# Multiplying output-projection slots in two 64-row halves of the array

## The chip, the cores and the metric

The kernel runs on one core of a Trainium2 chip. The metric is device time in microseconds (us) for one execution, the median of several runs.

## What is computed

A decoder trunk of four layers over 256 tokens of width 1024. Each layer has a token mixer (layers 0 and 3 a short gated convolution, layer 1 retention, layer 2 a chunked spatial gating), then a mixture of 16 experts of which each token uses two, then a gated embedding. All three mixers end in an output projection, a matrix product whose result is added to the layer's input:

```python
# layer 1, retention: VDIM = 2048 rows of w_out
o = o.reshape(bsz, seq, RET_VDIM).astype(x.dtype)
return (jax.nn.silu(g) * o) @ w_out
...
# layer 2, spatial gating: 3072 rows of w_out
vs = jnp.einsum("gts,bnsgd->bntgd", ws, v) + b_s.T[None, None, :, :, None]
return (u * vs.reshape(bsz, seq, SGU_HALF)) @ w_out
...
x = _layer_norm(ALPHA * x + mix, ln_g[i, 0], ln_b[i, 0])
ffn = _moe(x, router_w, router_b, moe_w_gate[i], moe_w_up[i], moe_w_down[i])
```

## The kernel before

**Tiling.** Tokens stand in two tiles of 128 (`T` = 2). Dense weights come in slots of 1 MB: 128 partitions by four quarters of 512 columns. A slot of an output projection holds 256 rows of `w_out`, as two chunks `j` of 128 rows, by 1024 columns, as two halves `c` of 512; quarter `2*j + c` is chunk `j`, half `c`. The retention layer's projection has 8 slots, the gating layer's 12, a convolution layer's 4.

**Precision by two parts.** Activations and weights are split into a high and a low part of type fp32r (`w_hi`, `w_lo`; for activations the pairs of views `oT`, `uvT`, `gT` in the buffer that the profile calls `work_r`). `product` (lines 635 to 639) makes one product from three matmuls: high by high (L637), high activation by low weight (L638), low activation by high weight (L639). The stationary operand is a 128x128 block of the activations, the moving one a quarter of the slot. The profile shows their types as f32.

**Sums.** The projection has four sums that run over all slots: PSUM bank `2*t + c` for token tile `t` and column half `c`. `rows_slot` works through one slot for one tile: 4 quarters x 3 matmuls. It starts the sums in slot 0 and ends them in the last slot, where it raises `half_done` and `mix_done`; for the second tile it raises `weights_used` with its last matmul, which frees the slot for the loads, casts and residues of later slots (SP, ScalarE L1248, VectorE L1556).

**Order.** The order on TensorE is written out by hand. In the retention layer (`retention_mixer`): slot 0 for both tiles, `rows_both` for slots 1 and 2, slot 3 for tile 0, transposes of later heads, slot 3 for tile 1, `rows_both` for slot 4, then `last_rows` for slots 5 to 7, tile by tile. In the gating layer (`sgu_mixer`), for q = 0 and 1: slot 4q for both tiles, `rows_both` for slot 4q+1, four spatial products (L927), `rows_both` for slot 4q+2, slot 4q+3 for tile 0, transposes, slot 4q+3 for tile 1; then `rows_both` for slot 8 and `last_rows`. `rows_both` is thus called for eight slots. It runs `rows_slot` for tile 0 and then for tile 1. `slot` (line 630) waits until the slot's low part is there.

**Other matmuls.** The expert products (`pair_product`, L1033) put two experts side by side on two column halves of the array: 64 columns of operand each, results on 64 PSUM partitions each, in plain f32. The gathers (L1025) are full-array matmuls of type fp32r with 256 moving columns. The scatter products (L1043, `put_back`) are full-array fp32r matmuls with 512 columns. L872 is retention's inner product, full-array f32. L648 is the transposes.

Of the kernel before, what the change touches and what calls it, by code (L numbers as in the profile page):

```python
# [5 lines left out]
P = 128  # L6
D = 1024
SEQ = 256
T = SEQ // P
# [16 lines left out]
HALF = 64  # L26
# [159 lines left out]
def build(nc, A, out):  # L186
# [9 lines left out]
    with ctx:  # L196
# [3 lines left out]
        def sem(name):  # L200
            return ctx.enter_context(nc.semaphore(name))
# [64 lines left out]
        psum = ctx.enter_context(nc.psum_tensor("psum", [P, 8, NB], F))  # L266
# [77 lines left out]
        weights_used = sem("weights_used")  # L344
# [2 lines left out]
        xt_in_psum, xt_ready = sem("xt_in_psum"), sem("xt_ready")  # L347
        x_half_ready, x_tile_ready, half_done = sem("x_half_ready"), sem("x_tile_ready"), sem("half_done")
        whole_used = sem("whole_slots_used")
        put_half, general_done = sem("put_half"), sem("general_path_done")  # L350
        norm_row, gate_norm_row, bias_row = sem("norm_row"), sem("gate_norm_row"), sem("bias_row")
        mix_done, mix_read = sem("mix_done"), sem("mix_read")
# [39 lines left out]
        def wait_over(eng, L, engine, step, r, p):  # L392
# [3 lines left out]
            eng.wait_ge(over[L][engine], n * PAIRS * r + n * p + OVER[engine].index(step) + 1)  # L396

        whole_slots = [proj for _, proj, _ in starts]
        places, load_order = zip(*expert_places())
        def expert_slot(L, k):  # L400
# [17 lines left out]
        def split_count(n):  # L418

            return n + 1 - QUICK - sum(proj < n for _, proj, _ in starts)  # L420
# [200 lines left out]
        @block.tensor  # L621
        def _(pe):
            mm = nc.tensor.matmul

            def quarters(n):

                return (w_hi[:, HIGH_OF[n], :].rearrange("p (j n) -> p j n", j=4),
                        w_lo[:, RAW_OF[n], :].rearrange("p (j n) -> p j n", j=4))

            def slot(n):  # L630

                pe.wait_ge(lo_ready, split_count(n))
                return quarters(n)

            def product(out, lhs, rhs, start, stop):

                mm(out, lhs[0], rhs[0], start=start, stop=False)  # L637
                mm(out, lhs[0], rhs[1], start=False, stop=False)  # L638
                return mm(out, lhs[1], rhs[0], start=False, stop=stop)  # L639

            def part(v, *at):
                return [a[at] for a in v]
# [93 lines left out]
            def rows_slot(n, count, lhs, q, t, i, done):  # L736


                s = 4 * q + i
                w = slot(n + s)  # L740
                order = [(j, c) for j in range(2) for c in range(2)]
                if s == count - 1:
                    order = [(j, c) for c in range(2) for j in range(2)]
                for j, c in order:
                    last = product(psum[:, 2 * t + c, :], part(lhs, ALL, 2 * s + j, t),
                                   part(w, ALL, 2 * j + c), s == 0 and j == 0, s == count - 1 and j == 1)
                    if s == count - 1 and (j, c) == (1, 0) and done is not emb_in_psum:
                        last.then_inc(half_done, 1)
                if t == 1:
                    last.then_inc(weights_used, 1)  # L750
                elif s == count - 1:
                    last.then_inc(done, 1)
# [4 lines left out]
                return [a.rearrange("p j (t n) -> p j t n", t=T) for a in v]  # L757

            def rows_both(n, count, lhs, s):
                for t in range(T):  # L760
                    rows_slot(n, count, lhs, s // 4, t, s % 4, mix_done)

            def last_rows(L, n, count, lhs):

# [74 lines left out]
            def retention_mixer(L):  # L839
# [63 lines left out]
                for i in range(1, 3):  # L903
                    rows_both(n, 8, tiled(oT), i)
# [3 lines left out]
                rows_slot(n, 8, tiled(oT), 0, 1, 3, mix_done)  # L908
                pe.wait_ge(oT_ready, 8)
                rows_both(n, 8, tiled(oT), 4)  # L910
                last_rows(L, n, 8, tiled(oT))

            def sgu_mixer(L):
# [35 lines left out]
                for q in range(2):  # L949
                    pe.wait_ge(mt_ready[L], 4 * (q + 1))  # L950
                    for t in range(T):
                        if q == 0:
                            pe.wait_ge(proj_ready[L], block_ready(5, t, 1))
                        rows_slot(n, 12, uvT, q, t, 0, mix_done)
                    rows_both(n, 12, uvT, 4 * q + 1)
                    spatial(q + 2)
                    rows_both(n, 12, uvT, 4 * q + 2)
                    rows_slot(n, 12, uvT, q, 0, 3, mix_done)
                    turn(q + 1)
                    rows_slot(n, 12, uvT, q, 1, 3, mix_done)  # L960
# [574 lines left out]
        def _(dve):  # L1535
# [99 lines left out]
            def layer_norm(t, k, banks_read=None):  # L1635

                rows_at, eps = (lambda c: psum[:, 2 * t + c, :], LN_EPS / ALPHA ** 2) if k % 2 else (
                    lambda c: x[:, t, c * NB:(c + 1) * NB], LN_EPS)

                dve.wait_ge(dve_step, steps[0])  # L1640
                if banks_read is not None:
                    dve.sem_inc(banks_read, 1)
                dve.wait_ge(lnp_loaded, 32 * (k + 1))

                def subtract_mean(i):
                    cols = slice(i * NB, (i + 1) * NB)
                    step(stt(x[:, t, cols], rows_at(i), nmv[:, 0, 0:1], ln_par[:, 0, cols],  # L1647
                             ALU.subtract, ALU.mult))

                [(_, rstd)] = moments([stats[:, t, 0:2, :]], subtract_mean, eps)  # L1650
                dve.wait_ge(dve_step, steps[0])
                for c, ready in enumerate((x_half_ready, x_tile_ready)):
                    cols = slice(c * NB, (c + 1) * NB)
                    stt(x[:, t, cols], x[:, t, cols], rstd, ln_par[:, 1, cols], ALU.mult, ALU.add).then_inc(ready, 1)
# [448 lines left out]
```

## Time and profile before

| | us |
|---|---|
| median of the timed runs | 1615.64 |
| lowest and highest of three | 1615.56, 1615.71 |
| span of the profiled execution, first to last instruction | 1613.2 |
| difference of the median and the span (launch and end) | 2.4 |
| TensorE busy in the span | 1600.2 |
| VectorE busy | 689.4 |
| ScalarE busy | 460.4 |

The profiled execution's own time is not listed beyond its span. A busy time of TensorE counts a matmul from its start to the end of its drain, and the next one starts before that end. The distance of starts tells what one costs. Weight loads have an engine row of their own, PEld.

### The profile page before, as it was taken

What the parts mean: (1) busy time and instruction counts of PE and PEld (TensorE: products, weight loads), DVE (VectorE), ACT (ScalarE), POOL (GpSimd) and SP (SyncE); (2) the same over time, 40 slices, a digit from 0 to 9 for tenths busy, and PEclk for the clock granted to TensorE, in tenths of its full rate; (3) what the DMA queues carried; (4) which work ended last, traced back from release to release, by engine and by line L of the source; (5) the groups of instructions that cost most, each with busy time, mean ns of one, the idle gap of its engine ahead of it and who ended that gap; (6) DMA issues with size and microseconds to landing.
All of it is one profiled execution on the core that took longest, in us unless ns stands there. A gap on an engine that the chain in (4) does not pass through costs nothing.

```text
span 1613.2 us, 17962 instructions
## 1 busy us (share of the span) xinstructions
PE 1600.2 (99%) x7576; PEld 961.3 (60%) x7584; DVE 689.4 (43%) x1023; ACT 460.4 (29%) x557; POOL 46.5 (3%) x47
## 2 busy tenths in 40 slices
PE   9999999999999999999999999999999999999998
PEld 7874433478877744433788888643434887444335
DVE  5671111294757711111956755511115767211117
ACT  5522111154433221111544433211102452211113
POOL 1000000010000000000110000000010000000000
PEclk9999999999999999999999999999999999999999
DMA  6989999946636799999557556999997388999992
GB/s 262 371 368 401 423 420 421 421 176 266 243 132 243 281 414 423 421 421 421 222 200 280 182 205 235 389 397 421 421 420 324 141 343 375 385 422 421 421 421 102
DMA packets 75146, 534.43 MB, mean 331 GB/s; under 512 B 8976, under 2 KB 9136, under 8 KB 10544
## 3 DMA queue, kind: packets, MB, share of 16 engines
q1 hardware_dynamic: 73728, 530.95, 81.2%
q0 software_dynamic: 1328, 2.21, 0.4%
q8 instruction: 65, 1.06, 0.3%
q14 instruction: 25, 0.20, 0.0%
HBM read 532.07 MB, written 1.05 MB: 330 GB/s over the span
## 4 chain that ended last, share of the span: by engine, by line
PE 90%; DVE 6%; DMA 3%; ACT 1%; issue 1%; SPq 0%; DVEq 0%; ACTq 0%
PE psum L1033 39%; PE psum L637 12%; PE psum L639 12%; PE psum L638 12%; PE psum L1025 4%; PE psum L648 3%; PE psum L1043 3%; DVE w_lo L1556 2%; PE psum L982 2%; DMA x<-in_experts 1%; DMA raw<-in_experts 1%; PE psum L975 1%; PE psum L927 1%; PE psum L872 1%; DVE x L1647 0%
## 5 line engine op out<-in xcount | busy, mean ns | idle before, releaser
L1556 DVE TENSOR_TENSOR w_lo<-raw,w_hi 128x2048 fp32r<-128x2048 f32 (+1 forms) x128 | 272.5, 2145 | 187.2 <-ACT w_hi L1248 186.7
L637 PE MATMUL psum<-w_hi,xT_hi 128*128 128x512 f32 x672 | 265.3, 395 | 3.0 <-DVE w_lo L1556 3.0
L1248 ACT ACTIVATE w_hi<-raw 128x2048 fp32r<-128x2048 f32 (+1 forms) x128 | 221.4, 1751 | 155.7 <-PE psum L639 113.1
L639 PE MATMUL psum<-w_hi,xT_lo 128*128 128x512 f32 x672 | 261.8, 390 | 0.0
L638 PE MATMUL psum<-w_lo,xT_hi 128*128 128x512 f32 x672 | 261.6, 389 | 0.0
L1248 ACT ACTIVATE work<-psum 128x512 f32<-128x512 f32 x152 | 85.8, 597 | 349.0 <-PE psum L648 247.3
L637 PEld LDWEIGHTS psum<-w_hi,xT_hi 128*128 128x128 f32 x672 | 126.2, 188 | 30.6 <-DVE w_lo L1556 4.5
L1033 PE MATMUL psum<-raw,xg 128*64 128x512 f32 x624 | 143.8, 594 | 0.0
L639 PEld LDWEIGHTS psum<-w_hi,xT_lo 128*128 128x128 f32 x672 | 126.1, 188 | 26.7
L638 PEld LDWEIGHTS psum<-w_lo,xT_hi 128*128 128x128 f32 x672 | 126.3, 188 | 25.8 <-issue 0.2
L1952 DVE TENSOR_REDUCE cg<-psum 128x1 f32<-128x256 f32 x32 | 13.6, 425 | 233.9 <-PE psum L1103 233.9
L1556 DVE TENSOR_TENSOR work_r<-psum,work_r 128x512 fp32r<-128x512 f32 x52 | 34.5, 688 | 183.7 <-ACT work_r L1248 183.7
L1248 ACT ACTIVATE xg<-psum 128x512 f32<-128x512 f32 x84 | 49.8, 597 | 203.3 <-PE psum L1025 102.1
L1033 PE MATMUL psum<-expert_work,xg 128*64 128x512 f32 x448 | 103.5, 594 | 0.0
L1033 PEld LDWEIGHTS psum<-raw,xg 128*64 128x64 f32 x624 | 43.9, 137 | 84.5 <-issue 83.9
L1033 PE MATMUL psum<-raw,work 128*64 128x512 f32 x400 | 92.9, 593 | 0.5 <-DMA raw<-in_experts 0.3
L637 PE MATMUL psum<-w_hi,work_r 128*128 128x512 f32 x224 | 89.2, 398 | 0.8 <-ACT work L1248 0.8
L639 PE MATMUL psum<-w_hi,work_r 128*128 128x512 f32 x224 | 87.6, 391 | 0.0
L638 PE MATMUL psum<-w_lo,work_r 128*128 128x512 f32 x224 | 87.5, 391 | 0.0
L1033 PE MATMUL psum<-expert_high,xg 128*64 128x512 f32 x336 | 79.5, 594 | 0.0
L1556 DVE TENSOR_TENSOR w_hi<-psum,w_hi 128x512 fp32r<-128x512 f32 x24 | 16.6, 692 | 141.7 <-ACT w_hi L1248 141.7
L1248 ACT ACTIVATE work_r<-psum 128x512 fp32r<-128x512 f32 x52 | 29.4, 600 | 159.7 <-PE psum L1033 156.2
(172 smaller groups left out, 1712.8 us busy)
## 6 DMA issues: line engine op xcount, KB each, us to landing
raw<-in_experts SPq DMA_DIRECT2D x128, 1024.0 KB, 15.9
raw<-in_slots SPq DMA_DIRECT2D x120, 1024.0 KB, 4.9
expert_work<-in_experts SPq DMA_DIRECT2D x88, 1024.0 KB, 15.4
expert_high<-in_experts SPq DMA_DIRECT2D x60, 1024.0 KB, 12.2
expert_spare<-in_experts SPq DMA_DIRECT2D x40, 1024.0 KB, 13.2
expert_bias<-in_experts SPq DMA_DIRECT2D x20, 1024.0 KB, 13.9
x<-in_experts SPq DMA_DIRECT2D x20, 1024.0 KB, 15.6
expert_norm<-in_experts SPq DMA_DIRECT2D x16, 1024.0 KB, 13.7
```

Source lines behind the costliest of these rows:

```text
L637: mm(out, lhs[0], rhs[0], start=start, stop=False)
L638: mm(out, lhs[0], rhs[1], start=False, stop=False)
L639: return mm(out, lhs[1], rhs[0], start=False, stop=stop)
L648: last = nc.tensor.transpose(psum[:, bank, i * P:(i + 1) * P], c, ident[:, :])
L872: last = mm(psum[:, 4 + k % 4, :], sT[:, h, (c + s) * P:(c + s + 1) * P], rv[:, s, h * DV:(h + 1) * DV], start=s == 0, stop=s == c)
L927: mm(tiles(psum[:, 4 + k % 4, 0:SVB]), sgu_wT[:, b // 2, :], sv[:, c, 3 * b:3 * b + 3, :], start=True, stop=True).then_inc(vs_in_psum, 1)
L982: last = mm(psum[:, 2 * t + c, :], pT[:, j, t * P:(t + 1) * P], whole[:, 2 * j + c, :], start=j == 0, stop=j == 1)
L1025: last = mm(psum[:, bank, j * SEQ:(j + 1) * SEQ], x_split[a][:, t, chunk], pick[:, t, Q * SEQ:(Q + 1) * SEQ], start=t + a == 0, stop=t + a ...
L1033: last = mm(psum[columns(e), bank, :], lhs(j, e), w[:, 2 * j + e, :], start=start and j == 0, stop=stop and j == 1)
L1043: last = mm(psum[:, bank0 + 2 * t + c, :], where[:, t * P:(t + 1) * P], what[i][:, c * NB:(c + 1) * NB], start=start and i == 0, stop=stop ...
L1248: return nc.scalar.activation(dst, src, func)
L1556: return tt(lo, whole, hi.bitcast(F), ALU.subtract)
```

## The change

`rows_both` no longer calls `rows_slot`. It splits each product by depth: the upper 64 partitions (rows of the array) and the under 64 are two matmuls with 128 output columns and 512 moving columns each. They are issued in turn, upper, under, upper, under, and at any time the two halves add to different sums (PSUM banks). A slot runs in four groups `k`. In group `k` the upper half adds to sum `k` of the list (c, t) = (0,0), (0,1), (1,0), (1,1), and the under half to sum `(k + 2) % 4`; after four groups every sum has had both halves. New waits keep the two halves from one sum: groups 0, 2 and 3 wait on the new semaphore `halves_done`, which TensorE itself raises at the end of groups 0 to 2, and group 1 waits on `weights_used` of the slot before, which group 3 (or a tile-1 `rows_slot`) raises.

```diff
         whole_used = sem("whole_slots_used")
+        halves_done = sem("row_halves_done")
...
             mm = nc.tensor.matmul
+            halves = [0]
...
             def rows_both(n, count, lhs, s):
-                for t in range(T):
-                    rows_slot(n, count, lhs, s // 4, t, s % 4, mix_done)
+
+                w = slot(n + s)
+                upper, under = slice(0, HALF), slice(HALF, P)
+                sums_of = [(c, t) for c in range(2) for t in range(T)]
+                for k in range(4):
+                    if k == 1:
+                        pe.wait_ge(weights_used, n + s)
+                    elif halves[0]:
+                        pe.wait_ge(halves_done, halves[0] - k // 2)
+                    for j in range(2):
+                        for x_part, w_part in ((0, 0), (0, 1), (1, 0)):
+                            for rows, (c, t) in ((upper, sums_of[k]), (under, sums_of[(k + 2) % 4])):
+                                last = mm(psum[:, 2 * t + c, :], lhs[x_part][rows, 2 * s + j, t],
+                                          w[w_part][rows, 2 * j + c], start=False, stop=False)
+                    if k < 3:
+                        last.then_inc(halves_done, 1)
+                        halves[0] += 1
+                    else:
+                        last.then_inc(weights_used, 1)
```

## Rows read from the trace of the kernel before

**Rows 1.** The page: span, TensorE's busy time, granted clock by slice, the chain's shares.
```profile
span 1613.2 us, 17962 instructions
...
PE 1600.2 (99%) x7576; PEld 961.3 (60%) x7584; DVE 689.4 (43%) x1023; ACT 460.4 (29%) x557; POOL 46.5 (3%) x47
...
PEclk9999999999999999999999999999999999999999
...
PE 90%; DVE 6%; DMA 3%; ACT 1%; issue 1%; SPq 0%; DVEq 0%; ACTq 0%
```

**Rows 2.** Chain that ended last, 500 to 552 us, retention's projection: start, us, what.
```profile
by line: PE psum L639 28.4%; PE psum L637 28.0%; PE psum L638 28.0%; PE psum L872 9.9%; PE psum L648 5.0%; PE psum L982 1.7%
...
500.05 5.15 PE psum L872 x12
...
524.30 1.75 PE psum L648 x16
```

**Rows 3.** Waits of TensorE in the whole run: us in total, times, longest.
```profile
PE psum L637 <- DVE w_lo L1556: 3.0, 6, 0.8
PE psum L669 <- POOL ones L577: 1.0, 1, 1.0
```

**Rows 4.** Groups by line and form: busy us, mean ns of one, idle before.
```profile
L1033 PE MATMUL psum<-raw,xg 128*64 128x512 f32 x624 | 143.8, 594 | 0.0
...
L637 PE MATMUL psum<-w_hi,work_r 128*128 128x512 f32 x224 | 89.2, 398 | 0.8 <-ACT work L1248 0.8
L639 PE MATMUL psum<-w_hi,work_r 128*128 128x512 f32 x224 | 87.6, 391 | 0.0
L638 PE MATMUL psum<-w_lo,work_r 128*128 128x512 f32 x224 | 87.5, 391 | 0.0
```

**Rows 5.** Timeline, TensorE, retention's projection (start, length): first and last of 64.
```profile
509.62 0.39 PE L639 MATMUL psum<-w_hi,work_r 128*128 128x512 f32 x1
...
523.90 0.40 PE L639 MATMUL psum<-w_hi,work_r 128*128 128x512 f32 x1
```

**Rows 6.** Timeline, TensorE, at 644.75 us: two gather matmuls, joint record.
```profile
644.58 0.40 PE L1025 MATMUL psum<-work_r 128*128 128x256 f32 x2
```

**Rows 7.** All gather matmuls: ns of one, least, median and most.
```profile
L1025 PE MATMUL psum<-work_r x512: 277/283/657, 116.0 to 1504.4; 128*128 128x256 f32 x171
```

**Rows 8.** Timeline around 513 us: product matmuls and their weight loads.
```profile
513.02 0.39 PE L639 MATMUL psum<-w_hi,work_r 128*128 128x512 f32 x1
513.03 0.19 PEld L637 LDWEIGHTS psum<-w_hi,work_r 128*128 128x128 f32 x1
513.25 0.39 PE L637 MATMUL psum<-w_hi,work_r 128*128 128x512 f32 x1
```

**Rows 9.** Timeline around 647 us: weight loads of the column halves.
```profile
646.98 0.14 PEld L1033 LDWEIGHTS psum<-expert_high,xg 128*64 128x64 f32 x2 [0.29 <-issue]
647.41 0.14 PEld L1033 LDWEIGHTS psum<-expert_high,xg 128*64 128x64 f32 x2 [0.28 <-issue]
```

**Rows 10.** Timeline, TensorE, 309.3 to 310.2 us: full array, then column halves.
```profile
309.12 0.63 PE L1043 MATMUL psum<-xT_hi,work_r 128*128 128x512 f32 x2
309.68 1.08 PE L1033 MATMUL psum<-expert_high,work 128*64 128x512 f32 x4
```

**Rows 11.** Timeline, 316.2 to 317.4 us: column halves, then full array.
```profile
315.74 1.03 PE L1033 MATMUL psum<-x,work 128*64 128x512 f32 x4
316.69 0.30 PEld L1043 LDWEIGHTS psum<-work_r 128*128 128x128 f32 x2 [0.81 <-issue]
316.70 0.74 PE L1043 MATMUL psum<-work_r 128*128 128x512 f32 x2
...
317.28 0.40 PE L1043 MATMUL psum<-w_hi,work_r 128*128 128x512 f32 x1
```

## The prediction

> **What bounds the kernel now.** I read the page first: TensorE is busy for 99% of the span, the chain that ended last runs on TensorE for 90% of it, and no slice of the span shows less than full granted clock (2.4 GHz) [rows 1]. The time is therefore a sum of TensorE instructions, and a change in a matmul stage is worth what it does to the start-to-start distance of matmuls there. Then I read the chain inside the retention layer's output projection: every piece of it is TensorE [rows 2], and of the few waits that TensorE has in the whole run, the largest total is 3.0 us, 0.8 us at a time [rows 3]. No transfer, cast or copy stands before this stage that could end up setting its length, so a shorter or longer matmul stage is passed on to the end in full.
>
> The busy column is of no use here. One product matmul has a record of 0.39 us [rows 4], but the next one starts after less than that, since matmuls are pipelined. What counts is the distance of starts: 64 product matmuls start between 509.62 and 523.90, so one costs (523.90 - 509.62) / 63 = 0.2267 us [rows 5]. All product matmuls of the output projections, three times 224, have this shape [rows 4].
>
> What is in the 0.2267 us? A gather matmul has the same data type and half the columns (256): two of them have a joint record of 0.40 us [rows 6] and one alone, at the median, of 0.283 [rows 7], so their starts are 0.12 us apart. Twice the columns cost 0.107 us more; 512 columns then take 0.213 us and 0.013 us are left that do not depend on the width. That remainder, a gap at each change of stationary operand, is all that a rearrangement of the same multiplications can win. The weight load itself is hidden already: the load for the next matmul starts at 513.03, with the matmul that began at 513.02, and ends (0.19 us) before the next matmul at 513.25 [rows 8].
>
> **The change, part by part.** It touches only slots that go through rows_both: s = 1, 2, 4 of the retention layer and s = 1, 2, 5, 6, 8 of the gating layer, 8 slots in all. Each has 2 tiles x 4 quarters x 3 products = 24 matmuls now: 24 x 0.2267 = 5.44 us, and 8 slots 43.5 us, 2.7% of the span.
>
> *The matmuls.* Each becomes two of half the depth (64 of 128 partitions), with all 128 output columns and all 512 moving columns: 48 matmuls and 48 loads for a slot, in 24 pairs. A matmul's length is its moving columns, so halving the depth saves nothing by itself; the change lives on both halves of a pair running at once. The trace of before has no 64-row matmul. The nearest rows are the expert products, which split the array by columns (128*64): their loads come in twos at 646.98 and 647.41, so a pair takes 0.43 us [rows 9], and a full-array matmul of the same type takes 5.15 / 12 = 0.43 us too [rows 2]. Two column halves thus run wholly side by side. I take it that row halves do so too. Then a pair has 0.213 us of streaming, plus whatever gap each half has at its own change of operand. Each half still reads one operand and then 512 columns, as the whole array does now, so I keep the gap: 0.2267 us for a pair, 24 pairs a slot, change 0. The bounds: if the gap vanishes, as it seems to have in the column pairs (0.43 us, twice 0.213 for a type that streams at half the rate), 192 pairs x -0.0133 = -2.6 us. If nothing overlaps, 192 x +0.2267 = +43.5 us.
>
> *Going into and out of halves.* The column halves show what it costs to turn the array over. In: a matmul pair of line 1043 begins at 309.12, its second member at 309.12 + 0.63 - 0.40 = 309.35, so the next was due at 309.58; the first column pair comes at 309.68, and the second follows after 1.08 - 0.59 = 0.49 us instead of 0.43 (0.59 is the record of one such matmul [rows 4]). Together 0.10 + 0.06 = 0.16 us [rows 10]. Out: two pairs from 315.74 are through at 316.60, the next full matmul starts at 316.70, and two of them take 317.28 - 316.70 = 0.58 us where 0.46 is usual: 0.10 + 0.12 = 0.22 us, since the next operand can be loaded only after the change [rows 11]. One visit costs 0.38 us. The visits: retention slots 1 and 2 together, slot 4 alone; in the gating layer the spatial products stand between slots 1 and 2 and between 5 and 6, and slot 8 is alone. That is 2 + 5 = 7 visits, 7 x 0.38 = 2.6 us. The lower bound is 0 (row halves might not need the turnover), the upper one is about 0.5 us a visit, 3.5 us, as a 128-column load (0.19 us) must be awaited [rows 8] where the column half awaits a 64-column load (0.14 us) [rows 9].
>
> Here a page bears on it. The Trainium skill ("TensorEngine Tiling (Array Packing)", Key Properties) says that a change of the tiling mode, not of the tile, drains the engine. The column rows agree; no row shows a row split, and by the rule row halves pay as well, whereas without it this term is 0 and the time stays at 1615.6 us.
>
> *The waits.* A slot gets four: on halves_done before groups 0, 2 and 3, on weights_used before group 1. Behind them on TensorE stand only the slot's own matmuls, and behind those the release of the slot. Each asks for the end of the group before the last, and 12 matmuls (6 pairs, 1.36 us) issued in between cover it, against 0.39 us from the start to the end of a group's last matmul [rows 4]. I cost them at nothing. Without that cover one wait would be like a turnover outward, 0.22 us, and the 31 of them (the very first group has none) some 7 us.
>
> *Instruction rate.* A pair needs two loads and two matmuls in 0.2267 us, 0.057 us each. The densest rows are transposes, a load and a matmul in 1.75 / 16 = 0.109 us, 0.055 each [rows 2]; gathers, of the type that matters, need 0.12 us, 0.06 each [rows 6, 7]; two loads started back to back stand 0.30 - 0.19 = 0.11 us apart [rows 11]. This is the tight place, and a rival below.
>
> *What doesn't move.* weights_used still rises once at the slot's end, so raw loads, casts and residues start as now; mix_done and half_done come from slots not touched.
>
> Sum: 0 + 2.6 + 0 = +2.6 us. The profiled execution's span is 1613.2 us, 2.4 us under the median of the timed runs, 1615.64; the stage is added to both alike. **Forecast 1618.2 us**, +0.16%, which is within the 0.2% that a measurement of this kernel can tell from no change.
>
> **The rivals.**
>
> *A. The gap is hidden.* While one half changes its operand the other streams, and a pair takes 0.215 us, half of the 0.43 of a column pair [rows 9]. 192 x -0.0117 = -2.2 us; with the 2.6 us of turnovers 1616.0 us, without them 1613.4. For it: the column pairs show no gap. Against it: the two halves never wait for each other, so a gap in each half lengthens the pair; for that I put A below the forecast. The Trainium skill ("TensorE: Matmul & The Clock Gate", Part 3) has loads overlap with running matmuls only where their row groups differ, which speaks for A as the change alternates row groups. The trace differs from that rule: loads of the same rows overlap now [rows 8].
>
> *B. Loads and matmuls of the two halves queue on one path (slower).* If 0.12 us is not the gather's streaming plus gap but the least distance at which this data type can be loaded and started [rows 6, 7], a pair takes 0.24 us. Against it stand the transposes, whose rate would give 0.219 us for two [rows 2]. It decides as soon as two loads and two starts need more than 0.2267 us. 192 x 0.0133 = +2.6 us on top of the turnovers: 1620.8 us.
>
> *C. The halves don't run at once: the change doesn't do what it says.* The two halves of a pair write two different sums over all 128 partitions at the same time, which the column halves (64 partitions each) never do. If the engine takes them one after the other, 48 matmuls a slot at 0.2267 us add 43.5 us: 1661.7 us.
>
> **How the numbers follow.** Forecast 0.44, A 0.24, B 0.14, C 0.16; 0.02 for something not thought of. Below 1612.4 us would be faster by over 0.2%: even a vanished gap without turnovers (1613.1) does not reach it, so 0.02. Above 1618.9 is slower: B, C and a tenth of the forecast's chance (a turnover of 0.5 us): 0.34. The rest is 0.64. The range takes in A without turnovers and B with slightly dearer ones, 1613.4 to 1621.2, and leaves out C.
>
> **What would show it.** In the timeline of the changed kernel, matmuls of 64*128 in the retention projection: starts in twos with 0.2267 us between twos bear out the forecast, 0.215 A, 0.24 B, and single starts 0.2267 us apart C. The turnover shows where halves meet full matmuls: 0.1 us extra before the first and a first distance lengthened by 0.05 to 0.12. A stretch without a matmul inside a slot would show that a wait lacks its cover. I am wrong if halves do not overlap, or if the turnover of row halves is free.

## The result and the profile after

The changed kernel takes 1620.25 us (median of 16 runs) beside 1615.65 us for the kernel before, and the ratio of the runs on record is 1.0026, 95% interval 1.0018 to 1.0033, that is +4.2 us (2.9 to 5.3; the two medians differ by 4.6). In a second set it took 1619.89 beside 1617.09 us, ratio 1.0022 (1.0011 to 1.0033). It is a little slower, by about 0.2%, and the forecast was 1618.2 us.

The page after: TensorE is still busy for 99% of the span. In the chain VectorE's share has fallen and that of DMA has grown; most of DMA's are expert loads, and one piece of 6.9 us is the slot load that e6 and e7 below are about.

```profile
span 1616.7 us, 18351 instructions
...
PE 1601.8 (99%) x7768; PEld 959.5 (59%) x7776; DVE 686.2 (42%) x1023; ACT 460.5 (28%) x557; POOL 53.2 (3%) x47
...
PE 91%; DMA 5%; DVE 3%; ACT 1%; issue 1%; SPq 0%; ACTq 0%
```

The half matmuls by form (busy us, mean ns of one). 256 + 128 of 64 rows stand in place of 192 of 128 rows; one of them has a record as long as a full one of rows 4, 0.39 us:

```profile
L774 PE MATMUL psum<-w_hi,work_r 64*128 64x512 f32 x256 | 41.5, 393 | 0.7 <-DVE work_r L1575 0.7
...
L774 PE MATMUL psum<-w_lo,work_r 64*128 64x512 f32 x128 | 25.0, 387 | 0.0
```

The timeline of TensorE as the retention projection goes into halves (start, length, count). Compare rows 5 and 10:

```profile
510.03 0.39 PE L640 MATMUL psum<-w_lo,work_r 128*128 128x512 f32 x1
510.26 0.39 PE L641 MATMUL psum<-w_hi,work_r 128*128 128x512 f32 x1
510.58 0.50 PE L774 MATMUL psum<-w_hi,work_r 64*128 64x512 f32 x2
510.91 0.40 PE L774 MATMUL psum<-w_lo,work_r 64*128 64x512 f32 x2
...
513.23 0.62 PE L774 MATMUL psum<-w_hi,work_r 64*128 64x512 f32 x4
513.68 0.39 PE L774 MATMUL psum<-w_lo,work_r 64*128 64x512 f32 x2
513.91 0.62 PE L774 MATMUL psum<-w_hi,work_r 64*128 64x512 f32 x4
514.36 0.39 PE L774 MATMUL psum<-w_lo,work_r 64*128 64x512 f32 x2
514.59 0.62 PE L774 MATMUL psum<-w_hi,work_r 64*128 64x512 f32 x4
```

Each "x2" with a record as long as one matmul's (0.39 us) is a pair: both halves start together. From 513.23 to 514.59 six pairs start, (514.59 - 513.23) / 6 = 0.227 us a pair, what a full matmul took in rows 5. So the pair costs exactly what the whole did; nothing was won and nothing lost there.

And out of halves again, to be read beside rows 11:

```profile
521.16 0.39 PE L774 MATMUL psum<-w_lo,work_r 64*128 64x512 f32 x2
521.39 0.39 PE L774 MATMUL psum<-w_hi,work_r 64*128 64x512 f32 x2
521.70 0.50 PE L639 MATMUL psum<-w_hi,work_r 128*128 128x512 f32 x1
522.04 0.40 PE L640 MATMUL psum<-w_lo,work_r 128*128 128x512 f32 x1
...
524.35 0.40 PE L641 MATMUL psum<-w_hi,work_r 128*128 128x512 f32 x1
```

In: the first pair was due at 510.26 + 0.23 = 510.49 and came at 510.58 (+0.09); the second followed after 0.33 instead of 0.23 (+0.10). Out: due 521.61, came 521.70 (+0.09); the second after 0.34 (+0.11). Then both ways the distance is a little long for a while: the ten starts from 510.91 to 513.23 take 2.32 us and those from 522.04 to 524.35 take 2.31, where 2.27 is usual. This drift is no mark of the split. The kernel before has it behind 16 transposes, where the array stays whole: ten starts in 2.30 us.

```profile
526.12 0.39 PE L638 MATMUL psum<-w_lo,work_r 128*128 128x512 f32 x1
...
528.42 0.39 PE L639 MATMUL psum<-w_hi,work_r 128*128 128x512 f32 x1
```

**Where the time lies.** Both touched stages run from the first product of slot 0 to the first embedding matmul. Those two starts are the rows of the timeline from which every length below is taken. For the kernel before:

```profile
504.64 0.79 PE L637 MATMUL psum<-w_hi,work_r 128*128 128x512 f32 x1
...
551.29 0.59 PE L982 MATMUL psum<-raw,emb 128*128 128x512 f32 x1
...
941.00 0.39 PE L637 MATMUL psum<-w_hi,work_r 128*128 128x512 f32 x1
...
1015.91 0.59 PE L982 MATMUL psum<-raw,emb 128*128 128x512 f32 x1
```

For the changed kernel:

```profile
504.59 0.79 PE L639 MATMUL psum<-w_hi,work_r 128*128 128x512 f32 x1
...
552.96 0.59 PE L1001 MATMUL psum<-raw,emb 128*128 128x512 f32 x1
...
941.86 0.39 PE L639 MATMUL psum<-w_hi,work_r 128*128 128x512 f32 x1
...
1019.06 0.59 PE L1001 MATMUL psum<-raw,emb 128*128 128x512 f32 x1
```

Retention: 46.65 us before, 48.37 after. Gating: 74.91 before, 77.20 after. Together +4.0 us; the rest of the two spans differs by 0.5 us the other way. The same two lengths of every kernel that ran, each from its one profiled execution, beside the median time (us):

| kernel | retention | gating | time | ratio to before, interval |
|---|---|---|---|---|
| before | 46.65 | 74.91 | 1615.65 | |
| changed, first profile | 48.37 | 77.20 | 1620.25 | 1.0026 (1.0018 to 1.0033) |
| changed, second (e0) | 47.63 | 77.21 | 1619.89 | 1.0022 (1.0011 to 1.0033) |
| changed, third (e7) | 48.30 | 77.21 | 1625.95 | one run |
| whole depth (e1) | 46.65 | 74.91 | 1615.85 | 0.9996 (0.9985 to 1.0007) |
| upper halves only (e2) | 47.55 | 77.20 | 1617.73 | one run |
| more visits (e3) | 49.74 | 79.56 | 1624.59 | 1.0044 (1.0028 to 1.0061) |
| halves in blocks (e4) | 48.93 | 80.42 | 1625.64 | one run |
| quarters (e5) | 51.91 | 83.45 | 1635.68 | one run |
| residues first (e6) | 47.61 | 77.21 | 1620.46 | 1.0017 (1.0007 to 1.0027) |

e0, e1, e3 and e6 ran beside 1617.09 us for the kernel before, the single runs beside 1615.16. The total time also carries waits in other stages, which come and go from profile to profile; in e7 and e5 one of 2.6 us, 0.4 us in the others, fell into the last layer. The stage lengths carry one such wait alone (0.7 us in the retention stage, see e6 and e7), so the argument on the split goes by them.

One more stretch differs. Near the end of the last layer, between the last scatter matmul (ended at 1582.59) and the next matmul, TensorE stands idle in the changed kernel:

```profile
1584.28 0.59 PE L656 MATMUL psum<-const 128*128 128x512 bf16 x2 [1.69 <-issue]
```

From the end of that scatter matmul to the end of the span it is 32.43 us in before, e1 and e2, which have as many matmuls as before, and longer in all seven profiles of kernels that have more: 33.2 us in e0, 34.1 in the first profile and 34.4 in e7, all three of the changed kernel, at most 34.5 (e5). So the change seems to cost another 0.8 to 2.0 us there, outside of the stages that it touches. e2 has the split and its turnovers too, so the number of instructions is the likelier cause; but the profile doesn't show what TensorE waited for ("issue"), and no run was made for this question. In the first profile the two stages (+4.0 us) and this stretch (+1.6) come to 5.6 us, and the span grew by 3.5: the rest of it was 2.1 us shorter.

### The profile page after: what moved, and what is told of

It is laid out like the page before. It is cut to its first block, busy times and chain, and to the rows that moved or that the text cites. A ratio compares the mean times of both kernels' runs of the same rounds, so it can differ in the third digit from the quotient of the medians.

```text
span 1616.7 us, 18351 instructions
## 1 busy us (share of the span) xinstructions
PE 1601.8 (99%) x7768; PEld 959.5 (59%) x7776; DVE 686.2 (42%) x1023; ACT 460.5 (28%) x557; POOL 53.2 (3%) x47
## 4 chain that ended last, share of the span: by engine, by line
PE 91%; DMA 5%; DVE 3%; ACT 1%; issue 1%; SPq 0%; ACTq 0%
PE psum L1052 38%; PE psum L639 11%; PE psum L641 11%; PE psum L640 11%; PE psum L1044 4%; PE psum L1062 4%; PE psum L650 3%; PE psum L774 2%; DMA raw<-in_experts 2%; PE psum L1001 2%; PE psum L807 2%; DMA x<-in_experts 1%; DVE w_lo L1575 1%; PE psum L994 1%; DMA raw<-in_slots 1%; PE psum L946 1%
## 5 line engine op out<-in xcount | busy, mean ns | idle before, releaser
L1575 DVE TENSOR_TENSOR w_lo<-raw,w_hi 128x2048 fp32r<-128x2048 f32 (+1 forms) x128 | 269.1, 2119 | 191.1 <-ACT w_hi L1267 190.7
L1575 DVE TENSOR_TENSOR work_r<-psum,work_r 128x512 fp32r<-128x512 f32 x52 | 34.5, 688 | 184.4 <-ACT work_r L1267 184.4
L1044 PE MATMUL psum<-work_r 128*128 128x256 f32 x512 | 74.9, 295 | 0.0
L1044 PEld LDWEIGHTS psum<-work_r 128*128 128x128 f32 x512 | 64.9, 190 | 10.8 <-issue 7.3
L1052 PEld LDWEIGHTS psum<-expert_work,xg 128*64 128x64 f32 x448 | 31.5, 137 | 60.5 <-issue 59.6
```

The lines of the kernel that those rows point to most:

```text
L1044: last = mm(psum[:, bank, j * SEQ:(j + 1) * SEQ], x_split[a][:, t, chunk], pick[:, t, Q * SEQ:(Q + 1) * SEQ], start=t + a == 0, stop=t + a ...
L1052: last = mm(psum[columns(e), bank, :], lhs(j, e), w[:, 2 * j + e, :], start=start and j == 0, stop=stop and j == 1)
L1575: return tt(lo, whole, hi.bitcast(F), ALU.subtract)
```

## The experiments

**e0: the changed kernel once more.**

> The changed kernel once more, for a second profile beside the others of this set. Theory: in the retention layer's projection and in the gating layer's, the stretch from the first product of slot 0 to the embedding matmuls (before: 46.6 us and 62.9 us from the first product of the first slot) is longer than before by 1.0 us (2 visits) and 2.3 us (5 visits), 0.47 us for each visit to row halves. In the first profile the retention stage had grown by 1.7 us, as TensorE also waited 0.7 us there for residues on VectorE, behind a slot load that took 6.9 us. If that wait is chance, it is missing here and the total is 1619.2 us; if it belongs to the change, it is here again and the total is 1620 us.

(The 62.9 us for the gating stage in this text is a slip; by the rows above it is 74.9.) Measured: retention +0.98, gating +2.30 us, no wait before slot 4, 1.0022 in the ratio. So the seven visits (each one into the halves and out again) cost 3.28 us, 0.47 each, and the 0.7 us of the first profile are not always there.

**e1: full depth in the new order.**

```diff
-                            for rows, (c, t) in ((upper, sums_of[k]), (under, sums_of[(k + 2) % 4])):
-                                last = mm(psum[:, 2 * t + c, :], lhs[x_part][rows, 2 * s + j, t],
-                                          w[w_part][rows, 2 * j + c], start=False, stop=False)
+                            c, t = sums_of[k]
+                            last = mm(psum[:, 2 * t + c, :], lhs[x_part][:, 2 * s + j, t],
+                                      w[w_part][:, 2 * j + c], start=False, stop=False)
```

> Full-depth products in the changed kernel's order of sums, with all its waits and increments of halves_done: 24 matmuls a slot, one sum after the other. It undoes the halving alone. Theory (turning the array over is the whole cost, the waits are covered): TensorE's starts stay 0.2267 us apart through every slot and the time is that of before, 1615.6 us. Rival (the 31 waits, or the new order of the sums, cost): up to the changed kernel's 1620 us, with stretches between the groups of a slot in which no matmul starts.

Measured: both stages as long as before to 0.01 us, and 1615.85 us. In the timeline, no distance is longer than usual, also where a group ends and a wait stands:

```profile
511.69 0.62 PE L774 MATMUL psum<-w_hi,work_r 128*128 128x512 f32 x2
512.14 0.39 PE L774 MATMUL psum<-w_lo,work_r 128*128 128x512 f32 x1
512.37 0.62 PE L774 MATMUL psum<-w_hi,work_r 128*128 128x512 f32 x2
512.82 0.39 PE L774 MATMUL psum<-w_lo,work_r 128*128 128x512 f32 x1
```

The waits, the extra increments and the new order of the sums cost nothing. All of the loss in the two stages belongs to the halving.

**e2: one half alone.** It leaves out the products of the under 64 partitions in the eight slots.

```diff
-                            for rows, (c, t) in ((upper, sums_of[k]), (under, sums_of[(k + 2) % 4])):
+                            for rows, (c, t) in ((upper, sums_of[k]),):
```

> The changed kernel with the upper halves alone: in the eight slots the products of the under 64 partitions are left out, 24 matmuls of 64 rows a slot. Theory (the halves run side by side, and each has its own gap of 0.013 us at a change of operand): one half alone starts every 0.2267 us, and the two stages are as long as in the changed kernel (47.6 and 77.2 us); time about 1620 us. Rival (the gap comes from two halves sharing a path): the half alone starts every 0.215 us, the eight slots are 2.2 us shorter, about 1618 us.

Measured: 47.55 and 77.20 us, the changed kernel's lengths, with half of its multiplications gone. The timeline (start, length, count), once settled:

```profile
513.91 0.61 PE L774 MATMUL psum<-w_hi,work_r 64*128 64x512 f32 x2
514.37 0.39 PE L774 MATMUL psum<-w_lo,work_r 64*128 64x512 f32 x1
514.59 0.61 PE L774 MATMUL psum<-w_hi,work_r 64*128 64x512 f32 x2
```

Three matmuls in 514.59 - 513.91 = 0.68 us, 0.227 each. In the two stages the second half is free, and a half alone has the whole gap of 0.013 us. That is why rival A did not come about: the gap is each half's own, and a neighbour doesn't fill it.

**e3: the same multiplications, more visits.**

```diff
+                    if k == 2:
+                        for c, t in (sums_of[0], sums_of[2]):
+                            mm(psum[:, 2 * t + c, :], lhs[1][:, 2 * s + 1, t], w[0][:, 2 + c], start=False, stop=False)
                     for j in range(2):
                         for x_part, w_part in ((0, 0), (0, 1), (1, 0)):
+                            if k % 2 == 0 and (j, x_part) == (1, 1):
+                                continue
```

> The same multiplications, but in each of the eight slots two products of the sums (0,0) and (1,0) are taken out of the halves and run as two full-depth matmuls between groups 1 and 2. Per slot 22 pairs and 2 full matmuls instead of 24 pairs; the visits to row halves rise from 7 to 15 (retention 3 + 2, gating 10). Theory (a price for each visit, 0.47 us): 8 visits more, +3.8 us over the changed kernel, about 1624 us. Rival (a price for each pair of halves, 4.4 us / 192): 176 pairs, 1619.7 us.

Measured: 1624.59 us, ratio 1.0044, so the time follows the visits and not the pairs. Retention, less the wait of 0.7 us before slot 4 that this profile has too, is 2.4 us longer than before, gating 4.65: 7.05 us for 15 visits, 0.47 each, the price that e0 gave for 7. One of the added turnovers in the timeline:

```profile
513.09 0.39 PE L779 MATMUL psum<-w_hi,work_r 64*128 64x512 f32 x2
513.41 0.73 PE L773 MATMUL psum<-w_hi,work_r 128*128 128x512 f32 x2
514.07 0.51 PE L779 MATMUL psum<-w_hi,work_r 64*128 64x512 f32 x2
514.41 0.40 PE L779 MATMUL psum<-w_lo,work_r 64*128 64x512 f32 x2
```

From pair to first full matmul 0.32 us, two full matmuls until 514.07 in 0.66, the next pair 0.34 later: 1.32 us for four distances, where 0.91 is usual.

**e4: first one half, then the other.** (The waits and the groups stay.)

```diff
-                    for j in range(2):
-                        for x_part, w_part in ((0, 0), (0, 1), (1, 0)):
-                            for rows, (c, t) in ((upper, sums_of[k]), (under, sums_of[(k + 2) % 4])):
+                    for rows, (c, t) in ((upper, sums_of[k]), (under, sums_of[(k + 2) % 4])):
+                        for j in range(2):
+                            for x_part, w_part in ((0, 0), (0, 1), (1, 0)):
```

> The same 48 half matmuls a slot and the same groups, but within a group the six of the upper half come first and then the six of the under half, not in turn. Theory (matmuls start in program order, so only neighbours in that order can run side by side): of a group's 12 starts only those where the half changes fall together, 10 distances of 0.2267 us a group instead of 6; 8 slots x 4 groups x 4 x 0.2267 = +29 us over the changed kernel, about 1649 us. Rival 1 (the engine runs whichever half is free): as the changed kernel, 1620 us. Rival 2 (no overlap at all here): 48 distances a slot, +43.5 us, 1663 us.

Measured: neither the theory nor a rival, but nearest to rival 1. Retention is 1.30 us and gating 3.21 us longer than with halves in turn (e0), +4.5 us and not +29: 0.65 us for each of the seven visits, some three distances of 0.2267. The way in, in the timeline:

```profile
512.34 0.49 PE L774 MATMUL psum<-w_hi,work_r 64*128 64x512 f32 x1
512.67 0.39 PE L774 MATMUL psum<-w_lo,work_r 64*128 64x512 f32 x1
512.91 0.63 PE L774 MATMUL psum<-w_hi,work_r 64*128 64x512 f32 x3
```

Two matmuls start alone, 0.33 us apart; from 512.91 on more start than one half can run (x3 within 0.63 us). If matmuls started strictly in program order, the six of a half would have to go by before the first of the other, 10 distances a group. That is ruled out by the stage lengths. The Trainium skill ("TensorE: Matmul & The Clock Gate", Part 3) says that they do start and end in program order; for the starts of matmuls of different rows this run does not agree. How far one half can run ahead of the other was not measured.

**e5: quarters of 32 rows.**

```diff
+                    if k == 0:
+                        pe.wait_ge(weights_used, n + s)
+                    else:
+                        pe.wait_ge(halves_done, halves[0])
...
+                            for r in range(4):
+                                c, t = sums_of[(k + r) % 4]
+                                rows = slice(32 * r, 32 * r + 32)
+                                last = mm(psum[:, 2 * t + c, :], lhs[x_part][rows, 2 * s + j, t],
+                                          w[w_part][rows, 2 * j + c], start=False, stop=False)
```

> Four quarters of 32 rows instead of two halves: 96 matmuls and 96 loads a slot, each quarter on another of the four sums, in four groups. A sum goes from one quarter to the next at every change of group, so every group waits for the end of the one before, with nothing issued in between. Theory (loads and matmuls of different rows start within some 0.003 us of each other, as in the changed kernel): four matmuls start together every 0.2267 us, and what is added is a wait at each of 32 groups, about 0.3 us, +10 us over the changed kernel: 1630 us. Rival (the rate at which instructions are issued is the next bound, 0.055 us each as in the transposes): eight instructions take 0.44 us, 192 x 0.21 = +41 us on top, about 1670 us.

Measured: +5.3 and +8.5 us to before, 13.8 in all where the text expected some 13 (10 on top of the changed kernel's 3.3), and 1635.68 us in its one run. The timeline (start, length, count) shows fours, and where a group ends:

```profile
513.75 0.40 PE L775 MATMUL psum<-w_lo,work_r 32*128 32x512 f32 x4
513.99 0.63 PE L775 MATMUL psum<-w_hi,work_r 32*128 32x512 f32 x8
514.45 0.40 PE L775 MATMUL psum<-w_lo,work_r 32*128 32x512 f32 x4
514.68 0.97 PE L775 MATMUL psum<-w_hi,work_r 32*128 32x512 f32 x8
515.49 0.40 PE L775 MATMUL psum<-w_lo,work_r 32*128 32x512 f32 x4
```

Within a group, three fours start in 514.45 - 513.75 = 0.70 us: four loads and four matmuls in 0.23 us, 0.03 us an instruction. So the rate of loads and starts, rival B, is not a bound at twice the density of the change. From the second step of this group (513.75) to the second of the next (515.49) it is 1.74 us where six distances are 1.36: an uncovered wait costs 0.38 us. Waits of the weight loads on the end of TensorE's own matmuls (us in total, times, longest) are in this kernel alone, three a slot:

```profile
PEld psum L775 <- PE psum L775: 12.1, 24, 0.5
```

It is what the changed kernel's order of groups avoids.

**e6: residues first; e7: the wait once more.** In the first profile TensorE waited before slot 4 of the retention projection, for residues on VectorE:

```profile
528.87 0.39 PE L641 MATMUL psum<-w_hi,work_r 128*128 128x512 f32 x1
529.94 0.50 PE L774 MATMUL psum<-w_hi,work_r 64*128 64x512 f32 x2 [0.68 <-DVE work_r L1575]
```

The chain that ended last (start, us, what) goes back from there to a slot load:

```profile
516.37 6.86 DMA raw<-in_slots
...
523.25 1.92 ACT w_hi L1267
...
525.20 2.29 DVE w_lo L1575
527.49 2.40 DVE work_r L1575 x4
```

VectorE takes the residue of that slot before the four residues of the activations, so a late load holds up slot 4. e6 turns these two around:

```diff
-                for used in range(25, 28):
+                for used in range(25, 27):
                     split_behind(n + used)
                 for k in range(4, 8):
                     save_rest(k)
+                split_behind(n + 27)
                 split_behind(n + 28)
```

> The changed kernel with one step moved on VectorE: in the retention layer the residues of heads 2 and 3 (four instructions on work_r) go ahead of the residue of the slot that is split behind slot 3, for which VectorE had waited for a late slot load. Theory: TensorE's wait of 0.7 us before slot 4 is gone if it was there, and the retention stage is longer than before by 1.0 us only; total 1619.2 us or, if the slot's residue is then late for a later slot, as much lost there as won. Rival (the wait has another cause): the wait before slot 4 stays.

> The changed kernel a third time, for one question: whether TensorE waits 0.7 us before slot 4 of the retention projection. It did in the first profile (slot load of 6.9 us), not in the second. Theory (chance of the slot load's landing): either; the retention stage is 47.6 us without the wait and 48.3 us with it, and the gating stage 77.2 us in both cases.

The cast of that slot on ScalarE (timeline: start, length; in brackets the idle time before and what ended it) in the first profile of the changed kernel:

```profile
523.25 1.92 ACT L1267 ACTIVATE w_hi<-raw 128x2048 fp32r<-128x2048 f32 x1 [3.18 <-DMA raw<-in_slots]
```

In e0, released by TensorE and not by the load:

```profile
523.91 1.92 ACT L1267 ACTIVATE w_hi<-raw 128x2048 fp32r<-128x2048 f32 x1 [1.66 <-PE psum L774]
```

In e6:

```profile
523.82 1.92 ACT L1267 ACTIVATE w_hi<-raw 128x2048 fp32r<-128x2048 f32 x1 [2.44 <-DMA raw<-in_slots]
```

In e7:

```profile
524.39 1.92 ACT L1267 ACTIVATE w_hi<-raw 128x2048 fp32r<-128x2048 f32 x1 [3.04 <-DMA raw<-in_slots]
```

In the first profile, in e3 and in e7 the load came late and TensorE waited; e0 had the load in time and no wait; in e6 (and in e4, which has the old order) the load was a little late and there was no wait. The chain above shows the mechanism: the late load and the order on VectorE. e6 doesn't show that its order takes the wait away. Counted from the first product of slot 0, the cast began after 18.66 us in the first profile (TensorE idle for 0.68 us), 18.59 in e7 (0.61), 17.28 in e0 (none) and 18.00 in e6. By the first two, a cast at 18.00 would have cost 0.1 us at most in the old order too. In the whole time 0.7 us is too little to be seen. The load was issued only 0.26 us later than before, counted in the same way, but took 6.9 us (first profile) and 6.8 (e7) where it took 5.0 before and 5.2 in e0. Why is open: in before, e1 and e2 it was in time, but with one profile each that can be chance.

## Why the prediction came out as it did

*What bounds the kernel* was right as far as the runs can tell: the two stages grew by 4.0 us in the first profile and 3.3 in the second, and the whole, by the two ratios, by 4.2 and 3.6. That the stages are passed on in full is not shown to the last microsecond, as other waits moved by as much. That no transfer, cast or copy could set the length of the retention stage was wrong: one did, by 0.7 us (see below).

*The matmuls, change 0*: right to the last digit that the timeline shows. The step from column halves to row halves held (pairs start together), and so did the argument that the gap is each half's own (e2). Rival A had its price from the column pairs, whose type has no gap at full width either (0.43 us in rows 2 and 9), so they could not show one hidden. Rivals B and C are out: e5 starts twice as many instructions in 0.23 us, and e2 shows the second half to be free. But the added instructions were priced by their rate alone, and the idle stretch near the end of the span, 0.8 us in e0 and 1.7 in the first profile, stands only in the kernels that have more of them. The prediction had no term for it.

*Turnovers, 7 visits at 0.38*: the count was right (e3), the price too small. Measured 0.47, by the trace 0.20 in (0.16 predicted), 0.20 out (0.22) and some 0.05 to 0.09 that the prediction had left out: after a turnover, as after transposes, the matmuls of this type take ten starts to settle to 0.227 us. I had read the first two distances of rows 10 and 11 and then taken 0.46 as usual. The term is 3.3 instead of 2.6 us, within its stated bounds (0 to 3.5). The Trainium skill ("TensorEngine Tiling (Array Packing)", Key Properties) says that a change of tiling mode drains the engine. The two starts at each change that come 0.09 to 0.11 us late agree with it for row halves; the trace shows these distances, not the drain itself.

*The waits, nothing*: right (e1). e5 shows what the cover is worth, 0.38 us a wait, where the prediction had 0.22.

*What doesn't move*: wrong in part. Behind one slot release in the retention layer hung a load, a cast, a residue and at last TensorE itself: 0.7 us in two of three profiles of the changed kernel. The turnovers put that release off by 0.26 us; most of the delay is that the load itself took longer, which is not explained. The prediction had looked at who raises `weights_used`, not at how little room the residues had before slot 4.

*The sum*: 3.3 us of turnovers, 0.7 us in part, and the 0.8 to 2.0 us by which the end of the span is longer make 4.0 us (e0) to 5.9 us (e7), plus or minus what other waits did. The timed ratios say +0.22% and +0.26%. The forecast of +0.16%, called no measurable change, lay just under the line; a slower kernel, which the prediction gave 0.34, is what came, by little, and the time lies in the range. The likeliest mechanism was the right one, with a term that was a fifth too small and two that stood at nothing; that the total came within 2.1 us of the forecast is in part luck.

## What to carry to other kernels

Splitting a full-depth product over rows won nothing here: the halves run side by side, but each still streams all columns and pays its own change of operand. As the second half is free beside the first (e2), a split could pay where an array half would stand empty, which no run here shows, and then in few long stretches, since each visit, in and out, costs 0.47 us here. Two halves in turn on different sums need no stall if the wait asks for the group before the last. A change that adds instructions is also to be looked at far behind the stage that it touches.

## What the runs showed of the hardware that was not expected

- Two halves need not be issued in turn. With six of one half ahead of six of the other, the engine still ran them side by side but for some three starts a visit (e4: +0.65 us a visit, where starts in program order would have cost 4.1 us a visit on average, 29 us over seven).
- Four 32-row matmuls with their four loads started every 0.23 us (e5), 0.03 us an instruction, where the densest rows of before have 0.055.
- After a change between whole and split array, fp32r matmuls took 0.23 us on average for some ten starts before they settled at 0.227. After transposes on the whole array they do the same (before, 526.12 to 528.42).
- In the seven profiles of kernels with more matmuls, TensorE stood idle for 0.8 to 1.9 us near the end of the span without a releaser that the profile shows, and in the three with as many as before it did not.
